# Two attentions taken in pairs of heads, with fill work between scores and values, and one gate panel turned into fill

## The chip, the cores and the metric

One core of one Trainium2 chip runs the whole program in one launch. The metric is the time of one execution on the device, in microseconds (us), as the median of several runs. Engines are named as in the profile: PE is TensorE's matmuls, PEld its weight loads, DVE is VectorE, ACT ScalarE, POOL GpSimd, SP SyncE, which issues the weight transfers.

## What is computed

Two transformer layers follow each other on 256 tokens of width 1024, all in float32. The first mixes three branches (a causal attention called MLA here, a gated linear attention and an attention to a memory) and ends in a feed-forward part; the second has a windowed attention A and a global attention B. The attentions that the change touches are these:

```python
# layer 1, 8 heads, queries and keys of 128 + 64 columns, causal
q_full = concat([q_nope, q_pe]); k_full = concat([k_nope, k_pe])       # k_pe is shared by the heads
o_mla = causal_block_attention(q_full, k_full, v_mla, (128 + 64) ** -0.5)
y = gates[0] * o_mla + gates[1] * o_gla + gates[2] * o_mem
x = x + y @ w_o
# layer 2, 8 heads of 64 columns in each of A and B, 2 heads of keys and values; 256 own tokens and 256 of a context
proj = h @ w_in + b_in
o_a = _windowed_attention(rope(q_a), rope(k_a), v_a, k_a_c, v_a_c, sink)
o_b = _global_attention(rope(rms(q_b)), concat([rope(rms(k_b)), k_b_c]), concat([v_b, v_b_c]))
y = (sigmoid(gate_a) * (o_a @ w_branch_a) + sigmoid(gate_b) * (o_b @ w_branch_b)) @ w_out
```

The columns of proj are computed in seven panels of 512, IN0 to IN6: IN0 to IN2 hold queries, keys and values, IN3 to IN6 the logits of the gates.

## The kernel before

**Panels and units.** Each product with a weight matrix is cut into panels of 512 output columns, and a panel into units of two 128-row slices of the weights. A weight is split into a high and a low part: ACT writes `whi` (L1273), DVE `wlo` (L1692), and PE adds three products per slice and token tile, so that a unit is 12 matmuls of L735. Raw weights and both parts have rings of four slots; `ahead(pos)` in the streams of ACT and DVE says how far the splitting has got, three units ahead of `pos`.

**Attentions.** Scores go to two PSUM banks `scores0` and `scores1`. Everything that is transposed, and the product with the values, goes to two banks `turned0` and `turned1`, used in turn in the order that `t_names` lists; a use starts when the bank's use before has been read. Per step, PE computes scores, DVE takes maxima (`softmax`: L2307 and L2308, or L2158 to L2160), ACT the exponentials into `prob` (L1591, L1490), PE transposes them (L797), ACT copies the result to `probT` (L1311), PE multiplies with the values (L1155, L1015), and DVE divides by the sums (`weigh`: L2323, L2001).

**The order before.** `attend` takes one head (MLA) or one head and one tile of 128 tokens (A and B) per step. In PE's stream a step i is: the scores of step i + 1, then units of fill if there are any, then the transposes of step i, then the values of step i - 1. MLA has 8 steps with one unit of G00 and G01 each. A and B together are 32 steps, called AB, with 14 units of IN4, IN5, IN6 and BA0, BA1 (`ab_units`), one in about every second step. Half of the queries and keys lie in partitions 0 to 63, half in 64 to 127: a head's lane is `64 * (h % 2)`. The scores of MLA are a product over 128 partitions (L1007) and one over the 64 of the head's lane (L1008), those of AB one over 64 (L1147).

**Around them.** Ahead of AB PE computes IN0 to IN3, then turns A's keys and queries (L1116, L1128), waits for ACT's copies (`turned`), and starts the scores. B's queries and keys are squared by POOL (L670), summed and inverted by DVE (L2280, `ab_inverse`), multiplied and rotated by POOL (L675 and on), and turned by PE after steps 12 and 13. `biased` adds a panel's bias on DVE (L1724), `gate2_sigmoid` (L1568) follows on ACT for a gate panel; ACT loads a table (ACT_TABLE_LOAD) each time that it changes between exponential, sigmoid and square root.

## Time and profile before

| | |
|---|---|
| median of 3 runs | 1007.68 us (1006.29 to 1007.76) |
| profiled execution, its own time | 1008.62 us |
| its span in the trace | 1007.0 us |
| PE busy | 960.7 us (95%) |
| DVE busy | 746.1 us (74%) |
| ACT busy | 552.0 us (55%) |
| chain that ended last, by engine | PE 66%, DVE 11%, issue 11%, ACT 6% |

The page of the profile gives busy times and the chain of work that ended last. The views used below are the timeline (one row per group of like instructions in order of time), the table of stretches, and the waits. Matmuls overlap, so a duration of a PE row is longer than what the matmul costs in a row of others: the cost is read from the start of one row to the start of the next. The same holds, with smaller overlaps, on DVE and ACT.

### The profile page before, as it was taken

Reading aid. Unit: us, or ns where it says so; the run is one execution under the profiler, and the core shown is the slowest. Engines: PE = TensorE matmul, PEld = TensorE weight load, DVE = VectorE, ACT = ScalarE, POOL = GpSimd, SP = SyncE. Lnnn points to the kernel's source line nnn. Section 1 sums busy time; section 2 is a strip of 40 time slices with the busy share of each in tenths; the row PEclk is TensorE's granted clock in tenths of the full one; section 3 lists DMA queues with packets and bytes.
Section 4 is the critical chain, followed back from the end, with each engine's and each line's share of the span. In section 5 each row is a group of like instructions: output and inputs, shape, how many; then the busy total and the mean of one; then the engine's idle time right before and its main releaser. Section 6 shows DMA issues by size and latency. Waiting matters only on the chain.

```text
span 1007.0 us, 13819 instructions
## 1 busy us (share of the span) xinstructions
PE 960.7 (95%) x4652; PEld 769.6 (76%) x4652; DVE 746.1 (74%) x1090; ACT 552.0 (55%) x818; POOL 168.4 (17%) x250
## 2 busy tenths in 40 slices
PE   7999999998999899999999999999999799999996
PEld 6787787876767787888888887767777578777885
DVE  5787467876657778887678887656558879999956
ACT  6557645474756445555333435766644367777632
POOL 8000000217200000110112002450000223333300
PEclk9999999998979999999999999999999899999999
DMA  8685453865542156887689655211115445556571
GB/s 254 215 254 162 131 167 108 289 212 161 172 147 100 70 161 223 268 266 238 203 306 356 179 181 196 75 63 63 63 45 181 131 134 169 171 169 207 184 230 50
DMA packets 99746, 175.11 MB, mean 174 GB/s; under 512 B 8252, under 2 KB 36444, under 8 KB 99692
## 3 DMA queue, kind: packets, MB, share of 16 engines
q1 hardware_dynamic: 92460, 148.87, 46.2%
q0 software_dynamic: 7184, 25.50, 7.7%
q8 instruction: 32, 0.52, 0.2%
q14 instruction: 22, 0.18, 0.1%
q10 hardware_dynamic: 48, 0.04, 0.0%
HBM read 173.33 MB, written 1.05 MB: 173 GB/s over the span
## 4 chain that ended last, share of the span: by engine, by line
PE 66%; DVE 11%; issue 11%; ACT 6%; POOL 4%; DMA 1%; POOLq 0%; ACTq 0%; DVEq 0%; SPq 0%
PE acc L735 49%; DVE wlo L1692 3%; PE scores L1147 3%; PE turned L1155 3%; PE turned L797 2%; ACT whi L1273 1%; PE turned L771 1%; PE scores L1008 1%; PE scores L941 1%; DMA raw<-in_w_mem_kv 1%; POOL act_lo L704 1%; POOL work L701 1%; POOL conv L701 1%; PE scores L1007 1%; DVE turn L1747 1%
## 5 line engine op out<-in xcount | busy, mean ns | idle before, releaser
L1692 DVE TENSOR_TENSOR wlo<-raw,whi 128x1024 fp32r<-128x1024 f32 (+2 forms) x270 | 344.6, 1298 | 105.7 <-ACT whi L1273 97.1
L1273 ACT CAST whi<-raw 128x1024 fp32r<-128x1024 f32 (+2 forms) x270 | 273.3, 1030 | 183.1 <-PE acc L735 139.4
L735 PE MATMUL acc<-whi,lta_lo 128*128 128x512 f32 (+2 forms) x576 | 229.8, 399 | 4.3 <-DVE lta_lo L1732 3.2
L735 PE MATMUL acc<-wlo,lta_hi 128*128 128x512 f32 (+2 forms) x576 | 223.1, 387 | 0.0
L735 PE MATMUL acc<-whi,lta_hi 128*128 128x512 f32 (+2 forms) x576 | 223.0, 387 | 0.0
L735 PEld LDWEIGHTS acc<-whi,lta_lo 128*128 128x128 f32 x576 | 109.2, 190 | 39.7 <-issue 13.8
L735 PEld LDWEIGHTS acc<-wlo,lta_hi 128*128 128x128 f32 x576 | 108.9, 189 | 22.5
L735 PEld LDWEIGHTS acc<-whi,lta_hi 128*128 128x128 f32 x576 | 109.5, 190 | 19.8
L735 PE MATMUL acc<-whi,ltb_lo 128*128 128x512 f32 (+1 forms) x272 | 109.3, 402 | 8.5 <-DVE wlo L1692 4.4
L630 POOL DMA_DIRECT2D wm<-in_w_mod x48 | 34.4, 719 | 468.7 <-DVEq L1792 270.6
L735 PE MATMUL acc<-whi,ltb_hi 128*128 128x512 f32 (+1 forms) x272 | 105.7, 388 | 0.0
L735 PE MATMUL acc<-wlo,ltb_hi 128*128 128x512 f32 (+1 forms) x272 | 105.7, 388 | 0.0
L735 PEld LDWEIGHTS acc<-whi,ltb_lo 128*128 128x128 f32 x272 | 52.5, 193 | 24.6 <-DVE wlo L1692 7.1
L1311 ACT ACTIVATE probT<-turned 128x512 f32<-128x512 f32 (+1 forms) x44 | 25.3, 576 | 70.4 <-PE turned L797 70.2
L735 PEld LDWEIGHTS acc<-wlo,ltb_hi 128*128 128x128 f32 x272 | 52.4, 193 | 10.5
L735 PEld LDWEIGHTS acc<-whi,ltb_hi 128*128 128x128 f32 x272 | 52.6, 193 | 9.1
L735 PE MATMUL acc<-whi,ff_lo 128*128 128x512 f32 x128 | 50.7, 396 | 0.0
L735 PE MATMUL acc<-wlo,ff_hi 128*128 128x512 f32 x128 | 49.8, 389 | 0.0
L735 PE MATMUL acc<-whi,ff_hi 128*128 128x512 f32 x128 | 49.8, 389 | 0.0
L735 PE MATMUL acc<-whi,act_lo 128*128 128x512 f32 x88 | 34.5, 392 | 0.0
L735 PE MATMUL acc<-whi,act_hi 128*128 128x512 f32 x88 | 34.3, 389 | 0.0
L735 PE MATMUL acc<-wlo,act_hi 128*128 128x512 f32 x88 | 34.3, 389 | 0.0
(343 smaller groups left out, 1423.2 us busy)
## 6 DMA issues: line engine op xcount, KB each, us to landing
raw<-in_w_in SPq DMA_DIRECT2D x88, 512.0 KB, 4.3
wm<-in_w_mod POOLq DMA_DIRECT2D x48, 512.0 KB, 5.6
raw<-in_w_up SPq DMA_DIRECT2D x88, 256.0 KB, 3.2
raw<-in_w_up SPq DMA_DIRECT2D x32, 512.0 KB, 4.5
raw<-in_w_down SPq DMA_DIRECT2D x32, 512.0 KB, 5.2
raw<-in_w_down SPq DMA_DIRECT2D x44, 256.0 KB, 3.2
raw<-in_w_mem_kv SPq DMA_DIRECT2D x8, 512.0 KB, 5.6
raw<-in_w_o SPq DMA_DIRECT2D x8, 512.0 KB, 3.4
```

The source lines that it names most:

```text
L630: pool.dma_start(wm[:, k], rows(a["w_mod_2"], k)[:, :, bass.ds(COLS * c, COLS)])\
L701: pool.tensor_tensor(cv[:, 2:4], cv[:, 2:4], sig[:], ALU.mult).then_inc(ev("conv_prod"), 1)
L704: pool.tensor_tensor(lo, cv[:, 2:4], hi.bitcast(F32), ALU.subtract).then_inc(conv_mul, 1)
L735: ins = pe.matmul(acc[s][:, t, 0:n], lhs[part][:, kt0 + kk, tok], w[:, u % RING, kk, 0:n], start=(k == 0 and kk == 0 and j == 0), stop=(la ...
L771: ins = pe.transpose(bank[:, 256 * kk + P * t:256 * kk + P * t + P], src[:, t, c:c + P], ident[:])
L797: ins = pe.transpose(bank[:, P * j:P * j + P], prob[:, (STEPS[name][0] + i) % 2, P * j:P * j + P], ident[:])
L941: ins = pe.matmul(bank[:, P * h:P * h + P], lhs[:, h, tok], rhs[:, h, tok], start=True, stop=True)
L1147: return pe.matmul(bank[:, :], qT[br][lane, h // 2, P * t:P * t + P], kT[br][lane, h // GROUP, :], start=True, stop=True)
L1155: ins = pe.matmul(bank[:, 0:HD], pT[:, P * kt:P * kt + P], v[:, HD * (h // GROUP):][:, 0:HD], start=(kt == 0), stop=(kt == 3))
L1273: act.copy(whi[:, s, :, 0:n], raw[:, s, :, 0:n]).then_inc(hi_ready, 1)
L1311: act.activation(dst, tb[b][0:(parts or P), 0:n], ACT.Copy, scale=scale).then_inc(t_free[b], 1)
L1692: dve.tensor_tensor(wlo[:, s, :, 0:n], raw[:, s, :, 0:n], whi[:, s, :, 0:n].bitcast(F32), ALU.subtract)\
```

## The change

`attend` stays for the memory attention; MLA and AB use a new `attend_pairs` in all three streams. A pair is two heads 2hp and 2hp + 1, one in each half of the partitions, for AB with one tile of tokens: 4 pairs in MLA, 16 in AB. PE's order for a pair p is: the transposes of both heads, the scores of pair p + 1, the units of fill, the values of pair p. A pair's two products with the values share one bank. The numbers of fill units by pair are tables: in MLA 1 ahead of the first pair and then 2, 1, 2, 2; in AB 2 and then one for each pair. IN3 has moved from the row of panels ahead of the attention into AB's fill, so that AB now has 18 units inside; A's keys and queries are turned ahead of IN2's last unit. On DVE, `diagonals("gate1")`, the sums of squares for B and the small products for `x3c` have moved behind the first three pairs. No product, exponential or transfer is added or taken away.

```diff
@@ -130,8 +130,8 @@
-AB_KEYS, AB_QUERIES, AB_OUT = 12, 13, 18
-AB_GATE = 2
+AB_KEYS, AB_QUERIES, AB_OUT = 5, 6, 8
+AB_GATE = 1
...
-AB_FILL = ["IN4", "IN5", "IN6", "BA0", "BA1"]
+MLA_PAIRS, AB_PAIRS = H_MLA // 2, HEADS * T
+AB_FILL = ["IN3", "IN4", "IN5", "IN6", "BA0", "BA1"]
...
+def mla_units(j):
+    return (1, 3, 4, 6, 8)[min(j, MLA_PAIRS)]
+
+def ab_units(j):
+    return min((4 * KT + 2 * KT // 2) // UNIT - AB_LAST, j + 2)
...
+def pairs_t(name, n, extra={}):
+    out = []
+    for p in range(n):
+        out += [f"{name}.PT{2 * p}", f"{name}.PT{2 * p + 1}", f"{name}.O{p}"] + extra.get(p, [])
     return out
...
@@ TensorE @@
+            def attend_pairs(name, n, scores, blocks, values, fill_units, after=None):
+                def score(p):
+                    banks = [s_begin(f"{name}.{2 * p + e}") for e in range(2)]
+                    for ins, (_, full) in zip(scores(p, [bank for bank, _ in banks]), banks):
+                        ins.then_inc(full, 1)
+                score(0)
+                fill_units(0)
+                for p in range(n):
+                    for e in range(2):
+                        i = 2 * p + e
+                        b, k = S_USE[f"{name}.{i}"]
+                        pe.wait_ge(s_free[b], k + 2)
+                        bank, full = t_begin(f"{name}.PT{i}")
+                        for j in range(blocks):
+                            ins = pe.transpose(bank[:, P * j:P * j + P], prob[:, e, P * j:P * j + P], ident[:])
+                        ins.then_inc(full, 1)
+                    if p + 1 < n:
+                        score(p + 1)
+                    fill_units(p + 1)
+                    for e in range(2):
+                        b, k = T_USE[f"{name}.PT{2 * p + e}"]
+                        pe.wait_ge(t_free[b], k + 2)
+                    bank, full = t_begin(f"{name}.O{p}")
+                    values(p, bank).then_inc(full, 1)
+                    if after:
+                        after(p)
...
+            def mla_scores(p, banks):
+                last = [None, None]
                 for t in range(T):
+                    for e in range(2):
+                        pe.matmul(banks[e][:, P * t:P * t + P * (t + 1)], qnT[:, 2 * p + e, P * t:P * t + P],
+                                  knT[:, 2 * p + e, 0:P * (t + 1)], start=True, stop=False)
+                    for e in range(2):
+                        lane = slice(64 * e, 64 * e + 64)
+                        last[e] = pe.matmul(banks[e][:, P * t:P * t + P * (t + 1)], qrT[lane, p, P * t:P * t + P],
+                                            kpT[lane, 0:P * (t + 1)], start=False, stop=True)
+                return last
...
-            for c in (1, 2, 3):
-                panel(f"IN{c}", lta)
+            panel("IN1", lta)
...
-            turn_keys(0)
-            turn_queries(0)
+            for k in range(4):
+                if k == 3:
+                    turn_keys(0)
+                    turn_queries(0)
+                unit("IN2", k, lta)
             turned("kA.0", "kA.1", "qA.0", "qA.1")
...
+            def ab_scores(p, banks):
+                br, hp, t = ab_pair(p)
+                if p == AB_PAIRS // 2:
+                    turned("kB.0", "kB.1", "qB.0", "qB.1")
+                return [pe.matmul(banks[e][:, :], qT[br][64 * e:64 * e + 64, hp, P * t:P * t + P],
+                                  kT[br][64 * e:64 * e + 64, 2 * hp // GROUP, :], start=True, stop=True)
+                        for e in range(2)]
...
@@ ScalarE @@
+                for p in range(n):
+                    ahead(first + units(p))
+                    if p >= 1:
+                        b, k = T_USE[f"{name}.O{p - 1}"]
+                        act.wait_ge(t_full[b], k + 1)
+                    for e in range(2):
+                        t_out(f"{name}.PT{2 * p + e}", probT[:, e, 0:P * blocks], P * blocks)
+                    if between:
+                        between(p)
+                    if p + 1 < n:
+                        exp(p + 1)
...
@@ VectorE @@
+                for p in range(n):
+                    ahead(first + units(p))
+                    if p + 1 < n:
+                        softmax(p + 1)
+                    for e in range(2):
+                        b, k = S_USE[f"{name}.{2 * p + e}"]
+                        dve.wait_ge(s_free[b], k + 2)
+                        sums(2 * p + e, rows_of(p)[e])
+                    b, k = T_USE[f"{name}.O{p}"]
+                    dve.wait_ge(t_full[b], k + 1)
+                    for e in range(2):
+                        ins = weigh(2 * p + e, e, rows_of(p)[e][:, 8:10], tb[b])
+                    ins.then_inc(t_free[b], 1)
+                    if after:
+                        after(p)
...
-            biased("IN3", gate2[:, :, 0:COLS])
...
-            diagonals("gate1", 16)
             done(dve.memset(stat[:, 3, :], 1.0))
...
+                if i == 0:
+                    for t in range(T):
+                        dve.wait_ge(ev("ab_sq"), t + 1)
+                        norm_sums(t)
+                    var(stat[:, 2:4, :], HD).then_inc(ev("ab_var"), 1)
+                    diagonals("gate1", 16)
+                elif i == 1:
                     inverse("ab", stat[:, 2:4, :])
                     dve.sem_inc(ev("ab_inverse"), 1)
...
```

On PE inside A, behind a unit of fill, the kernel before has this (`turned` and `scores` are PSUM banks with their number; `prob` and `probT` are exponentials and their transposes):

```order
L797 MATMUL turned0<-ident_55,prob_71 128x128 x4
L1155 MATMUL turned1<-qkv_89,probT_72 128x64 x2
L1155 MATMUL turned1<-kvx_83,probT_72 128x64 x2
L1147 MATMUL scores0<-kT_a_92,qT_a_90 128x512
L797 MATMUL turned0<-ident_55,prob_71 128x128 x4
L1155 MATMUL turned1<-qkv_89,probT_72 128x64 x2
L1155 MATMUL turned1<-kvx_83,probT_72 128x64 x2
L1189 MATMUL turned0<-diag_86,ones_87 128x128 x4
L1189 MATMUL turned1<-diag_86,ones_87 128x128 x4
L1147 MATMUL scores1<-kT_a_92,qT_a_90 128x512
```

The kernel after has this on PE, from the end of one pair's values on:

```order
L1210 MATMUL turned1<-qkv_89,probT_72 128x64 x2
L1210 MATMUL turned1<-kvx_83,probT_72 128x64 x2
L837 MATMUL turned0<-ident_55,prob_71 128x128 x4
L837 MATMUL turned1<-ident_55,prob_71 128x128 x4
L1200 MATMUL scores1<-kT_a_92,qT_a_90 128x512
L1200 MATMUL scores0<-kT_a_92,qT_a_90 128x512
L746 MATMUL acc0<-whi_50,lta_lo_54 128x512
```

Before, each score matmul stands between transposes of single steps; now two of them, one to each bank, follow eight transposes, and a unit comes right after.

On PE at the start of MLA, the scores of the first two heads before (`arena` holds queries and keys):

```order
L1007 MATMUL scores1<-arena_77 128x128
L1008 MATMUL scores1<-arena_77 128x128
L1007 MATMUL scores1<-arena_77 128x256
L1008 MATMUL scores1<-arena_77 128x256
L1007 MATMUL scores0<-arena_77 128x128
L1008 MATMUL scores0<-arena_77 128x128
L1007 MATMUL scores0<-arena_77 128x256
L1008 MATMUL scores0<-arena_77 128x256
```

The same two heads after:

```order
L1047 MATMUL scores1<-arena_77 128x128
L1047 MATMUL scores0<-arena_77 128x128
L1051 MATMUL scores1<-arena_77 128x128
L1051 MATMUL scores0<-arena_77 128x128
L1047 MATMUL scores1<-arena_77 128x256
L1047 MATMUL scores0<-arena_77 128x256
L1051 MATMUL scores1<-arena_77 128x256
L1051 MATMUL scores0<-arena_77 128x256
```

Before, products over 128 and over 64 partitions alternate for one head; now they come in twos, one for each head.

On DVE in the first two steps of A, before (`oab` and `qT_b` hold the squares for B):

```order
L2280 TENSOR_REDUCE stat_74<-oab_96 128x8
L2280 TENSOR_REDUCE stat_74<-qT_b_91 128x2 x2
L2307 TENSOR_TENSOR scores1<-scores1,keep_past_56 128x128
L2308 TENSOR_REDUCE soft_75<-scores1 128x1
L2311 TENSOR_SCALAR soft_75<-soft_75,gains_76 128x1
L2317 TENSOR_TENSOR soft_75<-soft_75 128x1
L2318 RECIPROCAL soft_75<-soft_75 128x1
L1692 TENSOR_TENSOR wlo_51<-raw_49,whi_50 128x1024
L2323 TENSOR_SCALAR oab_96<-turned1,soft_75 128x64
L2280 TENSOR_REDUCE stat_74<-oab_96 128x8
L2280 TENSOR_REDUCE stat_74<-qT_b_91 128x2 x2
L1769 TENSOR_SCALAR stat_74<-stat_74 128x32
```

On DVE behind the first pair of A, after (`diag` are the diagonals of gate1, which before were made ahead of the first maxima):

```order
L2422 TENSOR_SCALAR oab_96<-turned1,soft_75 128x64 x2
L2387 TENSOR_REDUCE stat_74<-oab_96 128x8
L2387 TENSOR_REDUCE stat_74<-qT_b_91 128x2 x2
L2387 TENSOR_REDUCE stat_74<-oab_96 128x8
L2387 TENSOR_REDUCE stat_74<-qT_b_91 128x2 x2
L1848 TENSOR_SCALAR stat_74<-stat_74 128x32
L2391 TENSOR_SCALAR diag_86<-ident_55,modc_60 128x128 x8
L1771 TENSOR_TENSOR wlo_51<-raw_49,whi_50 128x1024
```

Before, each tile's sums of squares stood behind a step of its own; now both tiles' and the diagonals stand in one row, ahead of the next split and the next maxima.

## Rows read from the trace of the kernel before

**Rows 1.** Busy times by stretch: us, then PE, PEld, DVE, ACT, POOL, clock, DMA

```profile
615.40:618.80 3.40, 2.12 (x18) 1.70 (x16) 2.88 (x9) 2.42 (x5) 0.00 (x0) 1.00 0.68 207
618.80:746.90 128.10, 127.06 (x668) 91.22 (x669) 77.47 (x203) 78.72 (x149) 24.96 (x40) 1.00 0.20 62
```

**Rows 2.** Timeline of PE, A: start us, us, engine, line, operation, count

```profile
638.07 0.60 PE L797 MATMUL turned<-ident,prob 128*128 128x128 f32 x4
638.50 0.56 PE L1155 MATMUL turned<-qkv,probT 128*128 128x64 f32 x4
...
639.43 1.12 PE L1147 MATMUL scores<-kT_a,qT_a 64*128 64x512 f32 x2
640.49 0.66 PE L797 MATMUL turned<-ident,prob 128*128 128x128 f32 x4
...
642.97 0.50 PE L735 MATMUL acc<-whi,lta_lo 128*128 128x512 f32 x1
...
645.83 0.60 PE L797 MATMUL turned<-ident,prob 128*128 128x128 f32 x4
```

**Rows 3.** Timeline of PE, memory attention, two heads one behind the other

```profile
97.90 1.14 PE L900 MATMUL scores<-arena 64*128 64x256 f32 x8
98.97 0.50 PE L735 MATMUL acc<-whi,lta_lo 128*128 128x512 f32 x1
```

**Rows 4.** Timeline of PE, memory attention, one head alone

```profile
110.57 1.13 PE L900 MATMUL scores<-arena 64*128 64x256 f32 x4
```

**Rows 5.** Timeline of DVE in A; in brackets idle time and what ended it

```profile
616.97 1.66 DVE L2286 TENSOR_SCALAR diag<-ident,modc 128x128 f32<-128x128 f32 x8
...
625.28 0.68 DVE L2280 TENSOR_REDUCE stat<-oab 128x8 f32<-128x512 f32 x1
...
626.63 0.30 DVE L2307 TENSOR_TENSOR scores<-scores,keep_past 128x128 f32<-128x128 f32 x1
...
628.21 1.22 DVE L1692 TENSOR_TENSOR wlo<-raw,whi 128x1024 fp32r<-128x1024 f32 x1
...
639.54 0.28 DVE L2323 TENSOR_SCALAR oab<-turned,soft 128x64 f32<-128x64 f32 x1 [1.45 <-PE turned L1155]
640.59 0.30 DVE L2307 TENSOR_TENSOR scores<-scores,keep_next 128x128 f32<-128x128 f32 x1 [0.77 <-PE scores L1147]
...
641.65 0.21 DVE L2311 TENSOR_SCALAR soft<-soft,gains 128x1 f32<-128x1 f32 x1
```

**Rows 6.** Timeline of ACT in A

```profile
618.55 1.28 ACT L1568 ACT_TABLE_LOAD   x1
619.84 1.06 ACT L1568 ACTIVATE gate<-gate 128x1024 f32<-128x1024 f32 x1
...
641.65 0.58 ACT L1311 ACTIVATE probT<-turned 128x512 f32<-128x512 f32 x1
...
643.54 0.29 ACT L1589 ACTIVATE soft<-gains,soft 128x1 f32<-128x1 f32 x1
...
644.41 1.04 ACT L1273 CAST whi<-raw 128x1024 fp32r<-128x1024 f32 x1
```

**Rows 7.** Timeline of PE in A, the rows of gate1

```profile
631.93 2.27 PE L1189 MATMUL turned<-diag,ones 128*128 128x128 f32 x16
```

**Rows 8.** Timeline of POOL on B: first and last of 40 instructions

```profile
642.85 1.04 POOL L675 TENSOR_TENSOR qkv<-qkv,stat 128x512 f32<-128x512 f32 x1 [29.59 <-DVEq L2334]
...
670.17 0.74 POOL L406 TENSOR_TENSOR work<-work 128x256 f32<-128x256 f32 x1
```

**Rows 9.** Timeline of PE, scores of one head of MLA and the unit behind

```profile
313.99 0.39 PE L1007 MATMUL scores<-arena 128*128 128x128 f32 x2
...
315.98 0.50 PE L735 MATMUL acc<-whi,lta_lo 128*128 128x512 f32 x1
```

**Rows 10.** Busy times by stretch at MLA's start, columns as in rows 1

```profile
285.30:295.60 10.30, 10.30 (x23) 6.35 (x23) 6.13 (x11) 3.12 (x6) 0.00 (x0) 0.50 0.36 124
```

193 lines of the change are left out of this document (98 added, 95 removed).

## The prediction

> **What bounds the kernel now.** I read the busy times by stretch first. In AB PE is busy 127.06 of 128.10 us at a clock of 1.00 while DVE and ACT work 77.5 and 78.7 us; ahead of it, from 615.4 to 618.8, PE is busy 2.12 of 3.40 us [rows 1]. So PE's own row of work sets the time, and the other engines count only where they let it wait: 1.0 us inside AB and 1.3 us ahead of it. The second view is PE's timeline, read from start to start. Two steps of A and a unit take 638.07 to 645.83, 7.76 us: transposes 0.43, values 0.93, scores 1.06 for one head, then the same again (transposes and values 1.42 together this time: 642.97 - 640.49 - 1.06), then a unit of 2.86 [rows 2]. The third is the question on which all rests, what two score matmuls in the two halves of the partitions cost together.
>
> **AB, scores.** The memory attention shows it. Its first two heads, one in each half, stand one behind the other: eight matmuls of 256 columns from 97.90 to 98.97, 1.07 us [rows 3]. One head alone, four such matmuls, lasts 1.13 against 1.14 for the eight [rows 4]. So the second half comes free. In AB a head's scores are two matmuls of 512 columns, as many columns as four of 256. A pair is bounded by 1.06 (all overlapped) and 2.12 (nothing); I take 1.06, the nearest row. 16 pairs x 1.06 = **-17.0 us**.
>
> **AB, joints.** Transposes and values of two steps cost 0.43 + 0.93 + 1.42 = 2.78 [rows 2]. In a pair they come as eight and sixteen matmuls in a row, with one change of kind fewer each. I estimate -0.1 for a pair, between 0 and -0.2: **-1.6**. The units are the same 2.86, only closer packed.
>
> **AB, waits that go.** A's keys and queries are turned ahead of IN2's last unit, whose 2.86 us cover ACT's four copies (0.5 each from start to start; 0.58 is one alone [rows 6]): **-1.3**. Without that cover it would be paid again. The 1.0 us inside AB ended on single steps' exponentials and goes too, since the new waits are counted in full below: **-1.0**.
>
> **AB, new waits.** (a) The second head's transposes need the bank that held the last pair's values, so they wait for DVE's `weigh`. DVE starts 0.11 behind the values (639.54 against 639.43) and two of 0.28 end at about 0.6 [rows 2, 5]; the first head's transposes cover 0.43. That is 0.2 x 15 = **+3.0**, between 1 and 5. Queued behind it on PE are the next scores, so nothing hides it.
>
> (b) From the start of a pair's scores to the next pair's transposes PE has 1.06 + 2.86 + 1.8 = 5.7 us, and 6.1 to those of the second head. DVE starts 1.16 behind the scores (640.59 - 639.43), takes 1.27 and 1.2 for the maxima (640.59 to 641.65 + 0.21), ACT follows with 0.87 for the second exponential (643.54 to 644.41) and 0.1 of signals [rows 2, 5, 6]: 4.7. The slack is 1.4 in A, and 2.4 in B, which has no mask and no sink. Whatever stands in between on DVE or ACT beyond this is paid.
>
> Behind pair 0 DVE has twice 1.35 of sums (625.28 to 626.63), 0.1, and the diagonals, 1.7: 4.5 [rows 5]. Less the slack of 1.4 and 0.2 that DVE is early, 2.9 are left, of which the 2.2 of gate1's rows on PE, which stand behind pair 1, hide most [rows 7]: **+0.7**. The sums of squares themselves waited for nobody before.
>
> Behind pairs 1, 5, 9 and 13 comes a gate panel. Counted from the end of the pair's values: `weigh` to 0.6, a split 1.2 [rows 5], the bias addition 1.2 (as wide as a split) to 3.05, ACT's sigmoid to 4.1, two copies to 5.1, the table of the exponential 1.28 to 6.4 [rows 6], two exponentials of B and the signal to 7.95. PE wants the second head's at 0.86 + 6.1 = 7.0. So about 0.95 at pairs 9 and 13; at 1 and 5, PE has gate1's rows or the turned keys in between, and 0.3 is left: **+2.2**. The table loads were there before; then each was hidden by the step ahead.
>
> (c) B's queries. POOL starts them when DVE has the inverse and ends 28.1 us later (642.85 to 670.17 + 0.74) [rows 8]. The inverse now comes behind pair 1, the queries are turned behind pair 6: five pairs of 6.7 = 33 us and the keys' turn. It costs nothing; 5 us of slack hide it.
>
> AB together: -17.0 - 1.6 - 1.3 - 1.0 + 3.0 + 0.7 + 2.2 = **-15.0 us**.
>
> **MLA.** One head's scores take 313.99 to 315.98, 1.99 us [rows 9], two heads 3.98. In the new order the products over 128 partitions follow each other without a change of kind, and of those over 64 the second head's overlap the first's. A pair saves at least 1.0 (those over 64 are half of 1.99) and at most 1.5; I take 1.3, three times: -4.0. The first pair runs at a clock of 0.50, which holds from 285.3 to 295.6 [rows 10]; there I estimate 2.1, between 1 and 3. Joints: -0.4. New waits: the bank, +0.5; and behind pairs 0 and 1 a chain as above. Behind pair 0: `weigh` and bias addition to 2.2 from the end of the values, sigmoid to 3.25, ACT's two casts for the splits to 5.35, the last split on DVE to 6.7, maxima of two heads (1.4 each, four instructions like those of rows 5) to 9.5, exponentials to 10.45, where PE is ready at 8.0: 2.45. Behind pair 1 DVE has two products over all of the branches (3.5), a split and a bias addition ahead of the sigmoid; ACT ends at 11.9, PE at 10.7 with its two units: 1.25. Together +3.7, between 1 and 6. MLA: -4.0 - 2.1 - 0.4 + 0.5 + 3.7 = **-2.3 us**.
>
> **Sum.** -17.3 us on the profiled execution's 1008.6 gives 991.3. Its time is 0.9 above the median of 1007.7, so the median comes to **990.4 us**.
>
> **Rivals.**
> 1. *The halves overlap, but in order.* A head's scores are two matmuls. If the second head's first could not start before the first head's second, a pair would be three matmuls of 0.43 ((1.06 - 0.2) / 2) instead of two: 0.43 x 16 = 6.9 and 0.7 in MLA, so 998.0. Against it: eight matmuls of 256 columns would then be seven of 0.21 and 0.2, 1.7 us, and the row shows 1.07 [rows 3]. The Trainium skill says this in "TensorE: Matmul & The Clock Gate", Part 3, "The mechanism": matmuls start and end strictly in program order. By that rule the time would be 998.0; the trace does not agree in its 1.07 us.
> 2. *Nothing overlaps*, the change doesn't do what it says: 0.86 more in each of 16 pairs and 1.6 in MLA, 990.4 + 13.8 + 1.6 = 1005.8. Rows 3 and 4 speak against it, unless 512 columns differ from 256.
> 3. *The waits of the pairs are larger.* DVE and ACT are in order and each pair has only 1.4 us of slack, where the old order had a whole step in hand. If each AB pair waits 0.5 more and MLA's two chains grow by 1, it is 990.4 + 8 + 1 = 999.4. For it: ACT and DVE work 78 us in 128, and in 111 that is 70%. Against: the cover of 5.7 us is longer than the chain of 4.7.
> 4. *PE's clock, slower than before.* PE ran at half its clock for 10.3 us at MLA's start [rows 10], which costs up to 5.2 us. If the waits behind the four gate panels each brought such a stretch into AB, it would be 20.6: 990.4 + 20.6 = 1011. It decides from 17.3 us, four such stretches. Against: AB's clock was 1.00 throughout, with stretches of two steps without a unit [rows 1, 2].
>
> **Chances.** Forecast 0.63 (984 to 997); better than 984, by smaller waits, 0.05; rival 1 0.08, rival 2 0.04, rival 3 0.17, rival 4 0.03. The range goes from 982 (new waits of 1.7 us instead of 10.1) to 1001, which takes in rivals 1 and 3 and leaves out 2 and 4 and some of either tail. Faster by over 0.2%, about what a measurement of this kernel can tell from no change, means below 1005.7: all but rival 4 and most of rival 2, 0.93; within 0.2% 0.03; slower 0.04.
>
> **What the profile after would show.** Right: AB's score rows with four matmuls in about 1.06 us to the next start; pairs of 6.5 to 6.8 us with a unit; no wait on ACT's copies ahead of the first scores; waits of PE on ACT's exponentials at the pairs behind gate panels, up to 1.5 us; POOL ready before PE turns B's queries. Wrong: score rows of 1.5 (rival 1) or 1.9 (rival 2); a wait on exponentials in every pair (3); a clock below 1.00 in AB (4); PE waiting for POOL behind pair 5 or 6. The likeliest error is in the new waits: they add up to 10.1 us (3.0 + 0.7 + 2.2 in AB, 0.5 + 3.7 in MLA), worked out from few rows.

## The result and the profile after

| | before | after |
|---|---|---|
| median (13 runs each, same chip) | 1007.55 us (1001.15 to 1009.59) | 999.46 us (996.44 to 1002.11) |
| ratio | | 0.9938, 95% interval 0.9919 to 0.9957 |
| span of the profiled execution | 1007.0 us | 997.9 us |
| PE busy in it | 960.7 us | 938.2 us |

By the medians the kernel is 8.1 us faster, where 17.3 were forecast; the ratio, 0.9938, says 6.2 us (4.3 to 8.2). The page of the kernel after, its span and PE's share, and the chain that ended last by engine:

```profile
span 997.9 us, 13803 instructions
...
PE 938.2 (94%) x4652; PEld 758.4 (76%) x4652; DVE 742.1 (74%) x1090; ACT 552.9 (55%) x819; POOL 166.4 (17%) x250
...
PE 58%; DVE 16%; issue 12%; ACT 7%; POOL 4%; DMA 1%; DVEq 0%; POOLq 0%; ACTq 0%; SPq 0%
```

PE lost 22.5 us of work and the span only 9.1; the rest is now waiting, and DVE's share of the chain rose from 11% to 16%. The busy times by stretch say where (columns as in rows 1; the first four rows are pairs 1, 2, 4 and 6 of AB, then all of AB, then MLA's start and all of MLA):

```profile
618.04:629.29 11.25, 9.07 (x58) 7.25 (x58) 9.40 (x31) 6.78 (x13) 0.81 (x1) 0.98 0.17 49
629.29:637.96 8.67, 8.41 (x42) 5.93 (x41) 5.60 (x13) 7.15 (x11) 7.81 (x12) 0.82 0.31 91
...
645.07:652.17 7.10, 6.81 (x43) 5.18 (x42) 4.70 (x13) 4.28 (x10) 6.39 (x9) 1.00 0.25 74
...
660.65:670.50 9.85, 8.34 (x49) 5.94 (x49) 5.70 (x14) 8.56 (x15) 0.00 (x0) 1.00 0.27 82
604.78:734.80 130.02, 122.50 (x706) 92.90 (x705) 80.99 (x213) 82.96 (x153) 29.46 (x46) 0.99 0.26 80
285.30:295.60 10.30, 9.81 (x51) 7.00 (x50) 6.27 (x17) 4.77 (x16) 0.00 (x0) 1.00 0.27 90
283.49:329.39 45.90, 42.36 (x233) 33.11 (x234) 29.69 (x59) 28.47 (x57) 0.00 (x0) 1.00 0.31 103
```

Against [rows 1] PE idles 7.5 us inside AB instead of 1.0. Against [rows 10] the clock at MLA's start is 1.00 instead of 0.50; whether the change did that is asked further below. I compare the two traces at fixed places of PE's work. The scores of MLA start 0.95 us earlier, with nothing changed ahead of them; MLA ends 7.0 earlier; the first unit of WO0 behind it only 3.9, the first of IN0 2.7; the second turn of AB's output 9.3 (737.58 against 746.92). So MLA won 6.0 us and gave most of it back, and AB won 6.7 where 15.0 were forecast.

A steady pair of A on PE and its `weigh` on DVE (start, us, engine, line, operation; in brackets the wait shown and what ended it). Behind `turned<-ident,prob`, the transposes, come scores, unit and values:

```profile
645.07 0.60 PE L837 MATMUL turned<-ident,prob 128*128 128x128 f32 x4
645.35 0.47 DVE L2422 TENSOR_SCALAR oab<-turned,soft 128x64 f32<-128x64 f32 x2 [1.32 <-PE turned L1210]
...
645.97 0.63 PE L837 MATMUL turned<-ident,prob 128*128 128x128 f32 x4 [0.29 <-DVE oab L2422]
...
646.53 1.13 PE L1200 MATMUL scores<-kT_a,qT_a 64*128 64x512 f32 x4
...
647.59 0.50 PE L746 MATMUL acc<-whi,lta_lo 128*128 128x512 f32 x1
...
650.44 0.55 PE L1210 MATMUL turned<-qkv,probT 128*128 128x64 f32 x4
...
652.17 0.60 PE L837 MATMUL turned<-ident,prob 128*128 128x128 f32 x4
```

The two heads' scores take 1.06 us to the next start, as one head's did [rows 2]. Read in narrow windows, two of the four matmuls start at 646.53 to 646.54 and two from 647.06 on, so they run in twos. The pair takes 7.10. What is long is the step from the first to the second head's transposes, 0.90 where four of them take 0.43 [rows 2].

Pair 1, DVE behind pair 0 and PE's rows of gate1:

```profile
621.51 1.67 DVE L2391 TENSOR_SCALAR diag<-ident,modc 128x128 f32<-128x128 f32 x8
...
624.47 0.29 DVE L2406 TENSOR_TENSOR scores<-scores,keep_past 128x128 f32<-128x128 f32 x1
...
627.61 0.48 DVE L2422 TENSOR_SCALAR oab<-turned,soft 128x64 f32<-128x64 f32 x2
...
625.13 1.11 PE L1244 MATMUL turned<-diag,ones 128*128 128x128 f32 x8
628.13 1.36 PE L1244 MATMUL turned<-diag,ones 128*128 128x128 f32 x8 [1.89 <-DVE oab L2422]
```

The second bank of gate1's rows waits 1.89 us for `weigh` of pair 1, which stands on DVE behind the sums, the diagonals, a split and the maxima of pair 2.

The tail of MLA, DVE's last `weigh` and splits, and PE's first unit of WO0:

```profile
329.66 0.75 DVE L2109 TENSOR_TENSOR arena<-turned,soft 128x256 f32<-128x256 f32 x2 [3.11 <-PE turned L1060]
330.33 2.35 DVE L1771 TENSOR_TENSOR wlo<-raw,whi 128x1024 fp32r<-128x1024 f32 x2
...
336.16 0.80 PE L746 MATMUL acc<-whi,lta_lo 128*128 128x512 f32 x1 [5.04 <-DVE lta_lo L1811]
```

DVE idles 3.11 us, then makes two splits ahead of the chain for which PE waits 5.04 us. In the kernel before this gap of PE is 3.73 us from the end of MLA, here 6.77.

### The profile page after: what moved, and what is told of

It reads as the page before. It is cut to its first block, busy times and chain, and to the rows that moved or that the text cites. A ratio compares the mean times of both kernels' runs of the same rounds, so it can differ in the third digit from the quotient of the medians.

```text
span 997.9 us, 13803 instructions
## 1 busy us (share of the span) xinstructions
PE 938.2 (94%) x4652; PEld 758.4 (76%) x4652; DVE 742.1 (74%) x1090; ACT 552.9 (55%) x819; POOL 166.4 (17%) x250
## 4 chain that ended last, share of the span: by engine, by line
PE 58%; DVE 16%; issue 12%; ACT 7%; POOL 4%; DMA 1%; DVEq 0%; POOLq 0%; ACTq 0%; SPq 0%
PE acc L746 46%; DVE wlo L1771 5%; PE turned L1210 2%; ACT whi L1326 2%; PE scores L1200 1%; PE turned L782 1%; PE turned L837 1%; DMA raw<-in_w_mem_kv 1%; POOL act_lo L715 1%; POOL work L712 1%; POOL conv L712 1%; PE scores L981 1%; DVE turn L1826 1%; PE turned L1101 1%; PE turned L947 1%
## 5 line engine op out<-in xcount | busy, mean ns | idle before, releaser
L746 PEld LDWEIGHTS acc<-whi,lta_lo 128*128 128x128 f32 x576 | 108.7, 189 | 45.2 <-issue 10.5
L746 PEld LDWEIGHTS acc<-wlo,ltb_hi 128*128 128x128 f32 x272 | 52.2, 192 | 10.5
```

The source lines that it names most:

```text
L746: ins = pe.matmul(acc[s][:, t, 0:n], lhs[part][:, kt0 + kk, tok], w[:, u % RING, kk, 0:n], start=(k == 0 and kk == 0 and j == 0), stop=(la ...
```

## The experiments

All start from the kernel after. "Time" is the median, and the ratio is to the kernel before, run in turn with it on the same chip; that kernel's own median moved between 1004.6 and 1006.9 from group to group, so small differences are read from the ratios and from stretches of the traces. A run is the median of 4 to 10 executions but has one trace only. Where AB's code is the same, AB took 132.8 us (kernel after), 133.3 (after_again), 133.3 (mla_in_turn) and 133.7 (mla_single), and 132.3 in split_before_weigh, whose edit touches AB only at its end. The first four have a stretch of about 3.4 us at a clock of 0.5 inside AB, split_before_weigh has none. So a difference of 1 us between two traces of AB is not a finding by itself.

| run | time, us | ratio, 95% interval |
|---|---|---|
| one_half | 1008.8 | 1.0033 (1.0011 to 1.0056) |
| scores_first | 997.3 | 0.9898 (0.9858 to 0.9937) |
| diag_ahead | 998.8 | 0.9922 (0.9893 to 0.9950) |
| gate_later | 999.6 | 0.9944 (0.9919 to 0.9970) |
| no_sigmoid | 998.9 | 0.9925 (0.9895 to 0.9955) |
| sigmoid_between | 998.0 | 0.9929 (0.9908 to 0.9949) |
| in3_ahead | 1008.5 | 1.0028 (1.0006 to 1.0051) |
| split_before_weigh | 995.6 | 0.9894 (0.9849 to 0.9939) |
| mla_in_turn | 1003.7 | 0.9979 (0.9958 to 0.9999) |
| mla_single | 997.9 | 0.9941 (0.9910 to 0.9973) |
| joined | 991.9 | 0.9869 (0.9821 to 0.9917) |
| joined_again | 992.8 | 0.9868 (0.9842 to 0.9895) |
| joined2 | 993.6 | 0.9870 (0.9826 to 0.9914) |
| joined_mla_single | 991.9 | 0.9866 (0.9831 to 0.9901) |
| after_again | 999.2 | 0.9933 (0.9909 to 0.9956) |

### Do the halves overlap?

```diff
-                return [pe.matmul(banks[e][:, :], qT[br][64 * e:64 * e + 64, hp, P * t:P * t + P],
-                                  kT[br][64 * e:64 * e + 64, 2 * hp // GROUP, :], start=True, stop=True)
+                return [pe.matmul(banks[e][:, :], qT[br][lane, h // 2, P * e:P * e + P],
+                                  kT[br][lane, h // GROUP, :], start=True, stop=True)
```

> The pairs of AB are the two tiles of tokens of one head, both in the same half of the partitions, instead of two heads in the two halves; order, fill, banks and waits as after. Theory: what a pair saves on scores comes from the halves alone. Score rows of four matmuls take 1.9 to 2.1 us to the next start instead of 1.06, 0.86 to 1.06 us more in each of 16 pairs: 999.5 + 13.8 to 17 = 1013 to 1016.5, slower than the kernel before. The scores are ahead of the fill, so no wait shrinks for it: the bank's wait stands ahead of them. Rival: the saving comes from the two banks or from larger numbers of like matmuls in a row: the rows stay at 1.06 and the time at 999.5.

The same row of PE, pair 4, with both products in one half of the partitions:

```profile
647.18 1.98 PE L1201 MATMUL scores<-kT_a,qT_a 64*128 64x512 f32 x4
649.09 0.50 PE L746 MATMUL acc<-whi,lta_lo 128*128 128x512 f32 x1
```

1.91 us instead of 1.06, and steady pairs of 7.95 instead of 7.10. So the halves alone give the 0.85; that two heads in one half take 1.91 and not twice 1.06 comes from standing in a row. Of 16 x 0.85 = 13.6 us only 10.5 show in AB (143.3 against 132.8 us from the first scores to the second turn of the output, the measure of AB in what follows), as pairs 1, 2 and 6 took the same time with longer scores (11.08, 8.52 and 9.87 us): their length is not set by PE. Without the overlap the kernel is slower than before.

### The wait for the bank

```diff
                         pe.wait_ge(s_free[b], k + 2)
+                        if e == 1 and p + 1 < n:
+                            score(p + 1)
                         bank, full = t_begin(f"{name}.PT{i}")
...
-                    if p + 1 < n:
-                        score(p + 1)
```

> PE computes the next pair's scores between the transposes of the pair's first and second head; nothing else is changed. Theory: in a steady pair of A the second head's transposes wait for the bank that DVE's weighing of the pair before still holds, and the two heads' transposes take 1.46 us from start to start where two runs of four take 0.86. So the wait is 0.60 in each of 15 pairs, 9 us in AB, and some 1.5 us in MLA. With 1.06 us of scores in between it is gone: steady pairs go from 7.10 to 6.5 us, the time from 999.5 to about 990. Rival 1: only the 0.29 us that the profile puts down to the weighing is a wait and the rest belongs to the transposes themselves: 15 x 0.29 = 4.4 us, to 995. Rival 2: ACT and DVE are the bound of a pair, and PE waits later, for the exponentials: no change in the 7.10 us.

The steady pair that answers to the one above, and pair 3, the second behind a gate panel:

```profile
647.63 0.60 PE L839 MATMUL turned<-ident,prob 128*128 128x128 f32 x4
648.17 1.13 PE L1200 MATMUL scores<-kT_a,qT_a 64*128 64x512 f32 x4
649.23 0.66 PE L839 MATMUL turned<-ident,prob 128*128 128x128 f32 x4
...
654.20 0.60 PE L839 MATMUL turned<-ident,prob 128*128 128x128 f32 x4
```

```profile
640.65 0.66 PE L839 MATMUL turned<-ident,prob 128*128 128x128 f32 x4 [0.26 <-ACT prob L1670]
641.60 1.13 PE L1200 MATMUL scores<-kT_a,qT_a 64*128 64x512 f32 x4 [0.29 <-ACT prob L1670]
```

654.20 - 647.63 = 6.57 us: the wait was 0.53 a pair, of which the trace had shown 0.29. AB got only 3.6 us shorter (129.2 against 132.8), not 8: pair 3 waits for ACT's exponentials instead (6.98 us against 7.11, with the two waits of the rows above), pair 6 is as long as before, and pair 1 grew from 11.25 to 11.89. The median fell by 2 us, the ratio by 0.0040, that is 4 us. AB's first scores came 2.2 us later than in the kernel after, and in this trace PE's clock was 0.5 from 313 to 316.4, inside MLA, where the kernel after has 1.00. The theory of the wait holds for steady pairs, the second rival for the others, and the time expected, 990, was not reached.

### Pair 1: what stands behind pair 0 on DVE

```diff
@@ diag_ahead @@
                     var(stat[:, 2:4, :], HD).then_inc(ev("ab_var"), 1)
-                    diagonals("gate1", 16)
...
+            diagonals("gate1", 16)
             done(dve.memset(stat[:, 3, :], 1.0))
@@ gate_later @@
-AB_GATE = 1
+AB_GATE = 7
...
-                    diagonals("gate1", 16)
...
+                if i == AB_GATE - 1:
+                    diagonals("gate1", 16)
```

> The eight diagonals of gate1 (1.7 us of DVE) are made ahead of the first maxima of A, as in the kernel before; all else as after. Theory: pair 1 lasts 11.25 us because DVE makes sums and diagonals for 4.5 us behind pair 0, so that the maxima of pair 2 and the weighing of pair 1 that stands behind them come late, the rows of gate1 wait 1.9 us for that weighing, and the wait is followed by a clock of 0.50 for 3.4 us. With 1.7 us less the wait falls to about 0.2 and the half clock goes: 1.7 + 1.7 = 3.4 us, 999.5 to about 996. Rival 1: the clock falls all the same, only 1.7 us are won (997.8). Rival 2: the diagonals now hold up the first maxima by as much, since PE waits for the first exponentials: no change in all.

> The diagonals of gate1 are made behind pair 6 and PE's rows of gate1 (2.27 us) follow pair 7; the sums of squares stay behind pair 0. In the run with the diagonals ahead of the first maxima they took 3.62 us instead of 1.66, while POOL squared B's queries, and the first pair got 0.8 longer as pair 1 got 2.0 shorter. Theory: behind pair 6 POOL rests and B has no mask, so they take 1.7 us and hold up nobody. Pair 1 goes from 11.25 to 7.8 us, pair 7 from 6.73 to 9.0: 1.2 us won, and the half clock of 3.4 us in AB goes with PE's wait, another 1.7: 999.5 to 996.6. Rival: without the rows as cover the waits behind pair 1 (table of the square root, bias, sigmoid) reach PE in full, pairs 1 and 2 together shrink by no more than the 2.27 us that pair 7 grows: 999.5.

In diag_ahead, DVE's diagonals, POOL beside them, and PE's first transposes:

```profile
605.25 3.62 DVE L2391 TENSOR_SCALAR diag<-ident,modc 128x128 f32<-128x128 f32 x8
605.25 1.04 POOL L681 TENSOR_TENSOR oab<-qkv 128x512 f32<-128x512 f32 x1 [41.29 <-DVE qkv L1803]
...
611.68 0.66 PE L837 MATMUL turned<-ident,prob 128*128 128x128 f32 x4 [1.10 <-ACT prob L1670]
```

Pair 1 fell from 11.25 to 9.28, gate1's rows waited for nothing, and the half clock behind them was gone. But the first maxima came late, PE waited 1.10 us for the first exponentials, so that pair 0 began 1.3 us later behind the first scores, and pair 0 itself took 0.8 longer. The net in AB is 0.2 us in the trace (132.6), 0.6 in the median, neither of which can be told from nothing: rival 2.

In gate_later pair 1 took 7.10, better than the 7.8 expected, and pair 7 with the rows 8.57. Pair 2 grew from 8.67 to 9.25:

```profile
627.77 0.63 PE L837 MATMUL turned<-ident,prob 128*128 128x128 f32 x4 [0.74 <-DVE oab L2422]
...
633.44 0.63 PE L1210 MATMUL turned<-qkv,probT 128*128 128x64 f32 x4 [1.03 <-ACT probT L1364]
```

AB was 1.7 us shorter in the trace (131.1; 1.2 shorter than split_before_weigh, which has no half clock in AB either), the time unchanged (999.6). The diagonals in the burst and the rows that waited for it were the cause of pair 1's length, since the sums of squares stayed where they were, but rows and diagonals have to stand somewhere, and part of the gain turned into waits at pair 2. The half clock of AB (0.52 from 629.1 to 632.5 in the kernel after) cost little there: with it pairs 1 and 2 took 11.25 and 8.67 us, without it, in split_before_weigh, 11.07 and 8.51. PE is held up there by others. That it was gone in diag_ahead and gate_later proves nothing for these edits: it was gone in split_before_weigh too, with pairs 0 to 14 unchanged, and back in after_again.

### Gate panels

```diff
@@ no_sigmoid @@
-                act.activation(gate2[:, :, c:c + COLS], gate2[:, :, c:c + COLS], ACT.Sigmoid).then_inc(gate_sig, 1)
+                act.activation(gate2[:, :, c:c + COLS], gate2[:, :, c:c + COLS], ACT.Copy).then_inc(gate_sig, 1)
@@ sigmoid_between: ACT, from behind the exponentials of pair p + 1 to behind the copies of pair p + 1 @@
-                if i in IN_DONE:
-                    gate2_sigmoid(IN_DONE.index(i))
...
+                if i - 1 in IN_DONE:
+                    gate2_sigmoid(IN_DONE.index(i - 1))
```

> The gates of layer 2 (IN3 to IN6) are copied on ACT instead of going through the sigmoid, so the output is another; this leaves out the table loads, twice 1.28 us behind each of the four gate panels. Theory: behind a gate panel ACT's row (sigmoid, copies, table, exponentials) is longer than PE's cover of a pair. Pairs 2, 6, 10 and 14 of the kernel after are longer by 0 to 2 us than the steady 7.10, and the two table loads, 2.56 us, are on the way to it in two of them: 2 to 3 us are won, 999.5 to 997. Rival 1: all four are paid in full, 4 x 1.28 = 5 us. Rival 2: the tables hide behind the units, and what is long in pairs 2 and 6 is the half clock and the order of ACT's copies: no change.

> ACT takes the sigmoid of a gate panel one place later, behind the copies of the next pair's transposes instead of ahead of them. In the kernel after, the copies of pair 6 end at 666.74 behind the sigmoid, and PE waits 0.71 us for them ahead of the values; those of pair 2 stand behind the sigmoid as well. Theory: the stall of a gate panel is one of ACT's order. The copies come 2 us earlier, pairs 2 and 6 lose 0.7 to 1.4 us each; the sigmoid and its two tables (3.6 us) now stand where ACT waits 1.6 us for DVE's maxima, and delay the exponentials by up to 2.0, of which 1.4 is slack. Sum -1.0 to -2.0, to 998. Rival: the delay moves in full from the values to the next transposes: 999.5.

The kernel after behind pair 5, ACT's sigmoid and copies and PE's wait for them:

```profile
664.72 1.06 ACT L1648 ACTIVATE gate<-gate 128x1024 f32<-128x1024 f32 x1 [1.12 <-DVE gate L1803]
665.68 1.06 ACT L1364 ACTIVATE probT<-turned 128x512 f32<-128x512 f32 x2
...
666.85 0.63 PE L1210 MATMUL turned<-qkv,probT 128*128 128x64 f32 x4 [0.71 <-ACT probT L1364]
```

no_sigmoid leaves out the sigmoid and with it the table loads of the gate panels. PE still waited 0.68 us for the copies in pair 2; pairs 2 and 6 lost 0.58 and 0.46 us, and AB 0.9 (131.9), or 0.5 against split_before_weigh. So the tables are at most about a tenth of what AB lacks. With the sigmoid behind the copies, pair 2 took 7.55 instead of 8.67 and pair 6 8.88 instead of 9.85, pair 3 0.2 more: AB 2.2 shorter in the trace (130.6; 1.7 against split_before_weigh), the time 1.4 less by the medians and 0.9 by the ratio. The stall is one of order on ACT: a sigmoid that waits for DVE's bias addition (the 1.12 above) stands ahead of copies that PE needs at once.

### IN3 as fill

```diff
-AB_FILL = ["IN3", "IN4", "IN5", "IN6", "BA0", "BA1"]
+AB_FILL = ["IN4", "IN5", "IN6", "BA0", "BA1"]
-    return min((4 * KT + 2 * KT // 2) // UNIT - AB_LAST, j + 2)
+    return (14 * (j + 1) + 8) // 17
```

> IN3 stands in the row of panels ahead of A again; A's keys and queries are turned ahead of IN3's last unit, and AB has 14 units of fill for 16 pairs and the start instead of 18, so that three places have none. Theory: a pair's chain (maxima and exponentials of both heads, 4.7 us, and the signals) is longer than what PE has without a unit (scores 1.06 and values 1.8, 2.9 us), so each place without a unit makes PE wait about 2 us: three of them 6 us, 999.5 to 1005.5. One gate panel less in AB gives back up to 1. So 1004.5 to 1005.5. Rival: the waits are filled by the other engines' slack; 999.5 as after.

Pair 7, which has no unit between its scores and its values:

```profile
679.21 1.13 PE L1201 MATMUL scores<-kT_b,qT_b 64*128 64x512 f32 x4
680.53 0.63 PE L1211 MATMUL turned<-qkv,probT 128*128 128x64 f32 x4 [0.19 <-ACT probT L1365]
...
682.36 0.66 PE L837 MATMUL turned<-ident,prob 128*128 128x128 f32 x4
683.59 0.63 PE L837 MATMUL turned<-ident,prob 128*128 128x128 f32 x4 [0.58 <-DVE oab L2425]
```

AB got only 2.3 us shorter (130.5) although four units, 10.9 us, had left it, so 8.6 us more of it are not this work; the time is 9.0 us longer. That is more than the 5 to 6 expected. The part was not where I had looked: pair 7 itself, in B, took 4.56 us and waited little, but pairs 1 and 13 took 11.95 and 7.23 us without a unit, as long as with one (11.25 and 7.10) or longer, since DVE and ACT set their length (PE waited 3.67 us for `weigh` in pair 1), and pairs 9 and 14 grew by 1.4 and 1.2. Nor are all 8.6 us waits: this trace has two half-clock stretches in AB (637 to 640.8 and 729 to 732.7), the second at the start of pair 14, where the kernel after has one. This is the half of the change that I had not priced by itself: work that fills waits is worth the waits.

### MLA and its tail

```diff
@@ split_before_weigh @@
                         sums(2 * p + e, rows_of(p)[e])
+                    if p + 1 == n:
+                        ahead(first + units(n))
                     b, k = T_USE[f"{name}.O{p}"]
@@ mla_in_turn @@
-                for t in range(T):
-                    for e in range(2):
+                for e in range(2):
+                    for t in range(T):
@@ mla_single: MLA's three streams and its uses of the banks as in the kernel before @@
-            attend_pairs("MLA", MLA_PAIRS, mla_scores, 3, mla_values, mla_fill)
+            attend("MLA", H_MLA, mla_scores, 3, mla_values, lambda i: fill(["G00", "G01"], i, 1))
```

> On DVE the last splits of an attention (two in MLA, one in AB) are made ahead of the last pair's weighing instead of behind it. In the kernel after DVE is idle for 3.11 us ahead of that weighing of MLA (329.66), then makes two splits (2.35 us), the bias addition, two copies and the low parts, and PE waits 5.04 us for them ahead of WO0. Theory: this is where MLA's gain of 6.0 us is given back; the chain gets 2.3 us shorter, PE waits 2.7 us, the time goes to 997.2. Rival 1: ACT's sigmoid and high parts are next on the chain, and less than 1 us is won. Rival 2: the shorter wait also takes away the half clock of 6.8 us that follows it: 2.3 + 3.4, to 993.8.

DVE and PE at MLA's end:

```profile
327.61 2.36 DVE L1771 TENSOR_TENSOR wlo<-raw,whi 128x1024 fp32r<-128x1024 f32 x2
330.62 0.76 DVE L2111 TENSOR_TENSOR arena<-turned,soft 128x256 f32<-128x256 f32 x2 [0.64 <-PE turned L1060]
...
334.85 0.50 PE L746 MATMUL acc<-whi,lta_lo 128*128 128x512 f32 x1 [2.77 <-DVE lta_lo L1811]
```

PE's wait fell from 5.04 to 2.77 us, the half clock behind it (0.51 from 335.5 to 342.4 in the kernel after) was not there, and the time fell by 3.9 us: the theory's 2.3 and part of the second rival's further 3.4. The clock's part is not firm. With this edit the stretch lasts 0 us here and about 3.4 in joined and joined_again; without it 6.8 in the kernel after and in after_again, but 3.4 in sigmoid_between and no_sigmoid, which leave MLA as it is.

> In MLA the two heads' scores are computed one head after the other, as before; pairs, fill and everything else as after. Theory: the twos are what saves in MLA: a pair's scores take 2.6 us in the kernel after, two heads in turn 3.98 before, so 1.4 us come back in each of three pairs at full clock and in the first one at the start: 4.2 to 5.6 us on PE. Part of it replaces waits of MLA's pairs (0.34 to 0.97 for the exponentials and the weighing), so 3 to 5 us: 1002.5 to 1004.5. Rival: the waits take it all, PE being held up by DVE's and ACT's rows of gate work anyway: 999.5 to 1000.5.

The scores of the second head in turn; those of a pair started at 291.75:

```profile
293.74 0.49 PE L1048 MATMUL scores<-arena 128*128 128x128 f32 x2
...
295.20 0.70 PE L1050 MATMUL scores<-arena 64*128 64x256 f32 x2
```

4.1 us for a pair instead of 2.65 (in the kernel after 290.44 to 293.09), and 4.2 us in the time, as expected: of four times 1.45, 5.8 us, most reaches the end.

> MLA takes single heads in the order of the kernel before; A and B stay in pairs. Theory: MLA's pairs won 6.0 us inside MLA, most of it because the half clock of 10.2 us at its start is not in the profile after, and the tail behind it (two splits, 2.3 us, and another half clock) gave 3 to 4 back. So undoing it costs 2 to 3 us: 999.5 to 1002, and the half clock of 10.2 us is back in MLA. Rival 1: the half clock comes and goes by itself; then it need not be there, and the kernel is at 999 to 1000. Rival 2: MLA's pairs are worth their whole 6 us: 1005.5.

Its profiled execution at MLA's start, columns as above:

```profile
285.00:296.00 11.00, 11.00 (x27) 6.87 (x26) 6.12 (x11) 3.62 (x7) 0.00 (x0) 0.53 0.37 130
```

The half clock is back, as [rows 10] has it. But it does not belong to the order of single heads. The kernel joined_mla_single, described below, has that order too, and its trace shows the full clock. The scores of MLA's second head, first in mla_single, then in joined_mla_single:

```profile
287.72 0.79 PE L1047 MATMUL scores<-arena 128*128 128x128 f32 x2
...
289.17 1.22 PE L1047 MATMUL scores<-arena 128*128 128x256 f32 x2
```

```profile
283.87 0.49 PE L1047 MATMUL scores<-arena 128*128 128x128 f32 x2
...
284.71 0.70 PE L1047 MATMUL scores<-arena 128*128 128x256 f32 x2
```

So two of the three traces with single heads have the stretch at MLA's start and one has not; none of those in pairs has it there, but scores_first and the joined kernels in pairs have one of 3.4 to 6.8 us further on in MLA. The times vary to match: seven of ten runs of mla_single took 995.1 to 1001.0 us at a mean granted clock of 0.984 to 0.990, and three, the profiled one among them, 1004.2 to 1005.3 at 0.979. The median is 997.9, that is, undoing MLA's pairs costs nothing that can be measured. The theory (1002) and the second rival are out. The kernel before, too, ran at 0.982 in the execution that was profiled and at 0.982 to 0.991 over all its runs. At one and the same clock, 0.986 to 0.987, the means are 1006.0 us before (14 runs), 998.8 after (8), 997.7 with MLA in single heads (3).

### The edits together

joined has the edits of scores_first, gate_later, sigmoid_between and split_before_weigh. joined_mla_single is the same with MLA in single heads. joined2 moves the bias addition on DVE as well:

```diff
                     if p + 1 < n:
                         softmax(p + 1)
+                    if between:
+                        between(p)
...
+                if i - 1 in IN_DONE:
+                    c = IN_DONE.index(i - 1)
+                    biased(f"IN{3 + c}", gate2[:, :, COLS * c:COLS * c + COLS])
```

> All of it in one kernel: scores of the next pair between the two heads' transposes, rows and diagonals of gate1 behind pairs 7 and 6, the sigmoid behind the copies, the last splits ahead of the last weighing. Theory: these are separate waits, so the gains add up as far as they don't touch: AB from 126.2 us (first transposes to the second turn of the output) to 122.6 by the scores (measured), and to about 120 by the two others, as both lie in pairs 1, 2 and 6, where the scores' change won nothing; 2.3 us more in MLA. 999.5 - 2.2 - 2.6 - 2.3 = 992.4. Rival: ACT bounds AB once the bank's wait is gone, and only MLA's part adds: 995.

> The kernel with all four edits (991.9), changed further: DVE adds a gate panel's bias between the next pair's maxima and its weighing, where it idles for some 3 us, instead of ahead of the maxima; ACT's sigmoid follows a pair later; half of the sums of squares are made in the first such gap, the diagonals of gate1 in that of pair 11, the rows behind pair 12. Theory: in the kernel with four edits pair 2 lasts 8.45 us and pairs 10 and 14 are 0.8 above the steady 6.57, since the bias (1.2 us) delays the maxima and the sigmoid the exponentials; in pair 2 PE waits 0.98 and 0.29 for exponentials. The gap takes the bias: pair 2 to 7.0, pairs 6, 10 and 14 shorter by 0.8 each: -3.5 us, to 988.4. Rival: ACT alone sets it (sigmoid and two tables, 3.6 us, against 1.8 it has idle): at most 1 us, 991.

> The kernel with the four edits, but MLA in single heads in the order of the kernel before (the edit on the last splits goes with the pairs of MLA, AB's loses its one). Theory: MLA's pairs are worth their cost only through PE's clock; single heads run at 0.979 or at 0.989 of the full clock, and take 1004.5 or 995.4 us with AB as after. So this kernel comes out in two groups 7 to 8 us below those, 988 and 997, its median by which group is larger; the kernel in pairs stays at 991 to 993. Rival: with the last splits ahead of the weighing MLA's pairs win 4 us at any clock, and this kernel is at 995 or slower throughout.

> The kernel with the four edits once more, beside the two others of this group. Both theories: 991 to 993, in one group.

> The kernel after, unchanged, beside them. Both theories: 998 to 1000, with a smaller spread than the kernel before (1001 to 1010), since the half clock at MLA's start that comes and goes with single heads is gone.

joined took 991.9 and 992.8 us in its two groups, 7 us less than the kernel after, with AB at 125.6 and 127.2 us. The two traces of this one kernel differ in pair 3, 6.98 and 8.60 us, where the second has a clock of 0.5 from 631.3 to 634.4: here, where PE sets the pace, such a stretch costs 1.6 us, where it cost 0.3 in the kernel after. With AB at 125.6 us, the three edits in AB give back 7.2 of the 8.3 us that AB lacks against the forecast (15.0 - 6.7). So most of the shortfall was in these waits. The kernel beats both others. What is left is in pairs behind gate panels, here ACT and PE in pair 2:

```profile
628.95 1.06 ACT L1648 ACTIVATE gate<-gate 128x1024 f32<-128x1024 f32 x1
...
630.02 1.28 ACT L1668 ACT_TABLE_LOAD   x1
...
632.33 0.66 PE L839 MATMUL turned<-ident,prob 128*128 128x128 f32 x4 [0.98 <-ACT prob L1670]
```

joined2 shortened pair 2 to 6.98 us and put the stall into pair 3, 8.52 us: there PE waited 0.86 us for DVE's `weigh` and then 0.85 for ACT's exponentials, which stand behind sigmoid and tables. Pair 4 took 8.58 us, but of that 1.7 is the clock:

```profile
640.37 2.01 PE L1200 MATMUL scores<-kT_a,qT_a 64*128 64x512 f32 x4 [0.29 <-ACT prob L1670]
```

The scores take twice their time. The run gained nothing (ratio 0.9870 against 0.9869), less than the 3.5 us of the theory and the 1 of the rival; that ACT alone sets the place, as the rival has it, is not shown. joined_mla_single took 991.9, so MLA's pairs are worth nothing measurable there either, with DVE's splits moved. Neither its theory nor its rival came: its six times do not fall into two groups, and the slowest alone is over 995. Its runs reached from 988.5 us (clock 0.989) to 998.7 (0.978), those of joined_again from 989.8 to 996.2 (0.986 to 0.982). after_again took 999.2 (997.3 to 1000.4).

## Why the forecast was right and wrong

The range and the direction held; the size was more than twice what came. The step that failed is AB's new waits. AB won 6.7 us where 15.0 were forecast; 0.8 of the 8.3 that it lacks stands ahead of its first scores, and 7.5 inside. So the new waits, put at 5.9 us (3.0 + 0.7 + 2.2), came to about 13.4 if the other terms held. By the forecast's own steps:

**AB, scores: right.** 1.06 us for both heads; one_half puts 0.85 of a pair on the halves, where rival 2 had 0.86. Rivals 1 and 2 are out. Rival 1 assumed that both matmuls of the first head stand ahead of those of the second. The trace has them in twos (646.53 and 646.54, then from 647.06), and that assumption does not agree with it. The rule cited there (the Trainium skill, "TensorE: Matmul & The Clock Gate", Part 3, "The mechanism") says that matmuls start and end in program order; starts in twos don't contradict it, and no run here shows which of them belongs to which head.

**AB, joints: right; the wait ahead: only in part.** Without its wait a pair takes 6.57 us, which is the forecast's sum (5.7 + 0.86). AB's first scores start at 604.78, 0.8 us later than the forecast's equivalent. From the turn of A's keys to the first scores PE took 3.38 us before and takes 5.68 now with a unit inside, so about 0.5 was won of the 1.3. The unit covers the copies of the queries, but the turn of the queries waits for ACT's copy of the keys, 0.91 us in the trace after (601.04) against 0.34 before (616.78); the profile after was to show no such wait.

**AB, new wait (a): too small, the largest error.** I put 0.2 a pair, 3.0 in all, and it is 0.53 in a steady pair, 8.0 if all 15 had it. The end of `weigh` was set at 0.6 us behind the values from a row in which it started 0.11 behind the start of the next work of PE. In the kernel after it starts 0.28 behind, ends at 0.75, and PE starts 0.15 after that. I had left out the way of the signal. How much of the 8.0 was really paid is less sure, since some pairs would have waited for ACT instead: taking the wait away shortened AB by 3.6 us (scores_first).

**AB, new waits (b): too small.** Pair 1 was to cost 0.7 beyond its rows. I took gate1's rows as cover for DVE's burst. They need the second bank themselves, and that waits for `weigh` of pair 1 at the end of the same burst. About 1.3 us more than forecast. Gate panels were to cost 2.2 in all; pairs 2, 6 and 8 are some 3.8 us longer than the forecast's pairs with their extras, beyond what (a) explains, pairs 9 and 13 some 1.6 shorter, which makes about 2 us more. I had followed the chain to the exponentials alone, and not to the copies of `probT`, which wait behind the sigmoid on ACT. 5.0 + 1.3 + 2 = 8.3, where 7.5 are missing inside AB: the total is measured, the split is rough, since the waits run into each other, and 5.0 is the upper end for (a).

**AB, (c), POOL: right.** POOL ended at 657.4, and PE turned the queries at 668.65 with no wait on it.

**MLA: near its net in the trace by errors that cancelled, and nothing in the time.** I had -2.3; the two traces differ by 1.7 from MLA's first scores to IN0, and mla_single, with a ratio of 0.9941 against 0.9938, shows no gain at all. The pairs save 1.45 us of scores each, as sized (1.3), and mla_in_turn shows it in the time. The new waits were put at 4.2 us and PE idles 3.5 in MLA (45.90 - 42.36), of which 2.3 is shown ahead of second heads' transposes, waiting for `weigh`; I had 0.5 for that and 3.7 for the chains. The half clock of 10.3 us [rows 10] was taken as given, and it is absent from the trace after: about 5 us that I had counted as staying, and that the change can't be credited with, as single heads run without it too (joined_mla_single). And the tail was not in the forecast at all: of a stage that is shortened I had priced every wait inside and none behind it. There the last splits stand behind `weigh`, where the old order had them one head earlier. It gave back 3.0 us, and a longer half clock more.

**Rival 3**, larger waits, had 0.17 and the number that came, 999.4. Its reason holds in part: each pair's slack is short and the queues are in order. But its sign, a wait on exponentials in every pair, did not show: steady pairs wait for the bank, 0.33 more than forecast and not 0.5, and MLA's two chains did not grow by 1: all of PE's idle time in MLA is 3.5 us. So its number is in part luck. That ACT or DVE were 70% busy was no use as evidence; the waits came from what stood ahead of what.

## What to carry to other kernels

When a saving on the bounding engine is certain, the forecast is decided by the waits that take its place: follow each new wait to the instruction that ends it, add the time that the signal takes, and ask whether the work named as cover needs the same resource. Price the stage behind a shortened one as well. Where engines wait for each other in order, fill work between a product and its use is worth the wait that it fills (here 9 us for four units), more than the place it had before.

## What was unexpected of the hardware

The table of waits gave 2.5 us in 9 waits for PE behind `weigh` in AB; taking the wait away changed a pair by 0.53 us where a row had shown 0.29. A PE wait after a matmul is shown too short, since the row's duration reaches past the point where the next could have started; start to start is the measure.

DVE's eight diagonals took 3.62 us with POOL multiplying beside them (diag_ahead, both from 605.25), 1.67 without. POOL's large multiplications took 1.04 us, as elsewhere. In the kernel after a small `tensor_scalar` of DVE (L2396, 8 columns) started at 606.39 inside a multiplication of POOL from 606.26 to 607.29 and took 0.93 us, that is to 607.32; in diag_ahead, started at 609.15 ahead of POOL's next at 609.20, it took 0.17. The Trainium skill says in "SBUF — State Buffer", "Who interferes with whom", that a `tensor_scalar` of DVE in a two-port mode and a GpSimd instruction lock each other out, and that the one issued first keeps the ports for its whole length. The 0.93 and 0.17 us agree with it; that these instructions ran in such a mode, no run here shows.

Same kernel, same chip: the mean granted clock of an execution ranged from 0.979 to 0.990 in mla_single, with 10 us between the ends. A stretch of half clock in one profiled execution is not a property of each run, nor of the order of the code around it (mla_single and joined_mla_single, joined and joined_again), and a forecast made against it should say so. What it costs depends on who sets the pace: 3.4 us of it cost 0.3 in pairs 1 and 2 of the kernel after, and 1.6 in pair 3 of joined_again.
